# x scaled once behind the sixth projection, and values and gates taken from PSUM by ScalarE

## What is computed

```python
u = rms_norm_2(h, norm_mix_g)                  # h * rsqrt(mean(h^2) + eps) * g
proj = u @ w_in                                # 1024 -> 3744 columns
conv_in, c_q, c_kv, k_rope_raw, gate_logits = jnp.split(proj, cut, axis=-1)
a, gt = jnp.split(conv_in, 2, axis=-1)
z = a * jax.nn.sigmoid(gt)                     # 512 channels, then 31 taps each
z = silu(layer_norm(depthwise_conv(z, conv_w) + conv_b))
conv_out = z @ w_conv_out
# c_q (384) and c_kv (256) are normed and projected to 8 heads' q, k, v
mla_out = causal_attention(...) @ w_mla_out
gates = jax.nn.sigmoid(gate_logits)            # 2 x 1024
h = h + (gates[0] * conv_out + gates[1] * mla_out) @ w_out
```

## Time and profile before

| | us |
|---|---|
| median of 3 runs (2503.04 to 2503.13) | 2503.06 |
| the profiled execution | 2503.1 |
| its span, first to last instruction | 2501.3 |
| TensorE busy | 2486.5 |
| VectorE busy | 1988.3 |
| ScalarE busy | 1244.2 |
| GpSimd busy | 305.2 |

### The profile page before, as it was taken

How to read it: one execution, slowest core, us unless ns; L and a number is a source line. 1 busy time by engine, 2 the same in 40 slices (tenths; PEclk the granted TensorE clock), 3 DMA queues, 4 the chain that set the end, 5 groups by cost and what they waited for, 6 DMA issues and landing times.

```text
span 2501.3 us, 36450 instructions
## 1 busy us (share of the span) xinstructions
PE 2486.5 (99%) x14212; PEld 2185.6 (87%) x14212; DVE 1988.3 (79%) x2830; ACT 1244.2 (50%) x1975; POOL 305.2 (12%) x250
## 2 busy tenths in 40 slices
PE   8999999999999999999999999999999999999998
PEld 7999988889999889999888899998888888888887
DVE  7878867778888688887777888876899786788873
ACT  6444444444444454444554544445577535654552
POOL 4000001220000000000023100000187221200002
PEclk9999999999999999999999999999999999999999
DMA  5333332233333323334323233334333333233331
GB/s 157 99 96 99 102 104 85 78 89 98 102 101 109 110 84 100 104 97 122 99 63 93 80 104 97 110 105 136 84 75 79 126 93 110 84 108 105 101 100 59
DMA packets 487297, 246.83 MB, mean 99 GB/s; under 512 B 42321, under 2 KB 483926, under 8 KB 486870
## 3 DMA queue, kind: packets, MB, share of 16 engines
q1 hardware_dynamic: 486674, 244.19, 33.9%
q10 hardware_dynamic: 452, 0.32, 0.0%
HBM read 240.27 MB, written 4.19 MB: 98 GB/s over the span
## 4 chain that ended last, share of the span: by engine, by line
PE 97%; DVE 1%; ACT 1%; DMA 0%; issue 0%; DVEq 0%; ACTq 0%
PE bank L893 8%; PE bank L892 8%; PE bank L891 8%; PE bank L774 6%; PE bank L775 6%; PE bank L776 6%; PE psS L913 5%; PE psS L914 4%; PE psS L915 4%; PE bank L1452 3%; PE psT L957 2%; PE psT L959 2%; PE psT L958 2%; PE psT L774 2%; PE psT L775 2%; PE psT L776 2%
## 5 line engine op out<-in xcount | busy, mean ns | idle before, releaser
L2267 DVE TENSOR_TENSOR wlo<-raw,whi 128x1024 fp32r<-128x1024 f32 (+2 forms) x212 | 288.8, 1364 | 49.8 <-ACT whi L1582 46.0
L774 PE MATMUL bank<-xhl,whi 128*128 128x512 f32 x672 | 264.5, 394 | 0.0
L775 PE MATMUL bank<-xhl,whi 128*128 128x512 f32 x672 | 261.9, 390 | 0.0
L776 PE MATMUL bank<-xhl,wlo 128*128 128x512 f32 x672 | 261.8, 390 | 0.0
L891 PE MATMUL bank<-xshl,whi 128*128 128x256 f32 x840 | 237.8, 283 | 0.0
L892 PE MATMUL bank<-xshl,whi 128*128 128x256 f32 x840 | 237.7, 283 | 0.0
L893 PE MATMUL bank<-xshl,wlo 128*128 128x256 f32 x840 | 237.7, 283 | 0.0
L1582 ACT ACTIVATE whi<-raw 128x1024 fp32r<-128x1024 f32 (+2 forms) x209 | 214.5, 1029 | 37.3 <-PE bank L776 22.2
L2330 DVE TENSOR_TENSOR wlo<-tw,whi 128x1024 fp32r<-128x1024 f32 x140 | 171.5, 1225 | 63.6 <-ACT whi L1622 63.5
L913 PE MATMUL psS<-hhi,whi 128*128 128x512 f32 x488 | 191.7, 393 | 0.0
L914 PE MATMUL psS<-hlo,whi 128*128 128x512 f32 x488 | 191.6, 393 | 0.0
(11 more groups left out here) (703 smaller groups left out, 7092.2 us busy)
## 6 DMA issues: line engine op xcount, KB each, us to landing
raw<-in_ffn_wg SPq DMA_DIRECT2D x88, 512.0 KB
raw<-in_ffn_wu SPq DMA_DIRECT2D x88, 512.0 KB
raw<-in_w_in SPq DMA_DIRECT2D x53, 512.0 KB
raw<-in_w_mlp SPq DMA_DIRECT2D x40, 512.0 KB
raw<-in_ffn_wd SPq DMA_DIRECT2D x48, 256.0 KB
raw<-in_ffn_wd SPq DMA_DIRECT2D x24, 448.0 KB
raw<-in_ffn_wd SPq DMA_DIRECT2D x48, 192.0 KB
raw<-in_ffn_wd SPq DMA_DIRECT2D x48, 128.0 KB
```

Source lines behind the costliest of these rows:

```text
L774: pe.matmul(dest, a, rhs_hi(k), start=start and k == 0, stop=False)
L775: pe.matmul(dest, a, rhs_lo(k), start=False, stop=False)
L776: mm = pe.matmul(dest, b_, rhs_hi(k), start=False, stop=stop and k == tiles - 1)
L2267: dve.tensor_tensor(wlo[:, a:a + n], raw[:, a:a + n], whi[:, a:a + n].bitcast(F32), ALU.subtract).then_inc(s_split, 1)
```

## The change

- Behind kr, the sixth projection, `x` gets its inverse root after all: GpSimd multiplies the eight chunks of `x` by `inv` into `gate_a`, ScalarE rounds them with the gain into `xhi` (`scaled_hi`, as soon as kr is through with that chunk), VectorE makes `xlo` (`scaled_lo`).
- a0 waits for `scaled_lo` chunk by chunk. From it on, results in PSUM are final.
- The 24 evictions of a, g and gates leave VectorE. ScalarE takes them out of PSUM: a Copy times 0.5 for values, the Tanh itself for gates and g. `s_ea` takes the place of `s_i2` for them. Some takes get further waits (for the use of their target by others).
- On VectorE the add of the kv latents' squares stands between `scaled_lo` 0 to 3 and 4 to 7, and these stand before the three `latent_norm` and the split of a1.
- In the slots ScalarE takes the slot's own unit behind the Exp and three tap products (from slot 15 on behind the layer norm's Silu and rounding), where it used to do the Tanh of the previous slot's.
- Semaphores of the first block's attention are used again in the cross attention and for `mem`, in place of seven of their own.

```diff
             in_unit("kv", 1)
             pe.wait_ge(s_i2, evicted("q", 0))
-            in_unit("kr", 0)
+            c = unit_of("kr", 0)
+            pe.wait_ge(s_split, c + 1 + RING)
+            for k in range(KC):
+                wh, wl = wcols(whi, c, k), wcols(wlo, c, k)
+                pe.matmul(bank_of[("kr", 0)], wh, chunk(xhi, k), start=k == 0, stop=False)
+                pe.matmul(bank_of[("kr", 0)], wh, chunk(xlo, k), start=False, stop=False)
+                pe.matmul(bank_of[("kr", 0)], wl, chunk(xhi, k), start=False, stop=k == KC - 1
+                          ).then_inc(s_kc if k < KC - 1 else s_used, 1)
             pe.wait_ge(s_gn, GN2)
             pe.wait_ge(s_v7, 8 + QC + KVC - 2)
             ones_sum(psS[:, 512:1024], [chunk(lsq, QC)]).then_inc(s_ss, 1)
             pe.wait_ge(s_i2, evicted("q", 1))
-            in_unit("a", 0)
+            in_unit("a", 0, ready=lambda k: pe.wait_ge(s_xsl, k + 1))
...
                 if s % 2 == 0 and h < H2:
-                    pe.wait_ge(s_i2, evicted(*FILL[s]))
+                    pe.wait_ge(s_ea, taken(*FILL[s]))
                     project(h, "k")
...
+            def take(kind, i):
+                act.wait_ge(s_used, unit_of(kind, i) + 1)
+                dest = {"a": tmp[i % 2][:, :], "g": tmp[2 + i % 2][:, :], "gate": gate[i]}[kind]
+                if kind in ("a", "g") and i >= 2:
+                    act.wait_ge(s_z, i - 1)
...
+                act.activation(dest, bank_of[(kind, i)], ACT.Copy if kind == "a" else ACT.Tanh, scale=0.5).then_inc(s_ea, 1)
+
+            def scaled_hi(k):
+                if k < KC - 1:
+                    act.wait_ge(s_kc, k + 1)
+                else:
+                    act.wait_ge(s_used, unit_of("kr", 0) + 1)
+                act.wait_ge(s_t, k + 1)
+                act.activation(chunk(xhi, k), chunk(gate_a, k), ACT.Copy,
+                               scale=gains[:, FINAL1 * KC + k:FINAL1 * KC + k + 1]).then_inc(s_xsh, 1)
...
             split(unit_of("kr", 0) + AHEAD, 0)
+            for k in range(KC):
+                scaled_hi(k)
             for j in range(QC):
                 latent_hi(j)
...
                 products(some)
-                if s >= 3:
-                    i = s - 3
-                    act.wait_ge(s_i2, evicted("gate", i))
-                    act.activation(gate[i], gate[i], ACT.Tanh, scale=0.5).then_inc(s_gt, 1)
-                elif s == 2:
-                    glu_tanh(3)
                 if s:
                     products(some)
+                if s < LN_Y:
+                    take(*FILL[s])
...
+            def scaled_lo(k):
+                dve.wait_ge(s_xsh, k + 1)
+                dve.scalar_tensor_tensor(chunk(xlo, k), chunk(gate_a, k), gains[:, FINAL1 * KC + k:FINAL1 * KC + k + 1],
+                                         chunk(xhi, k).bitcast(F32), ALU.mult, ALU.subtract).then_inc(s_xsl, 1)
...
             newton(LATQ, acc)
             evict("kv", 1)
+            for k in range(KC // 2):
+                scaled_lo(k)
+            dve.wait_ge(s_lq, QC + KVC)
+            dve.tensor_tensor(chunk(lsq, QC), chunk(lsq, QC), chunk(lsq, QC + 1), ALU.add).then_inc(s_v7, 1)
+            for k in range(KC // 2, KC):
+                scaled_lo(k)
             for j in range(QC):
                 latent_norm(j)
             split(unit_of("kr", 0) + AHEAD, 0)
-            dve.wait_ge(s_lq, QC + KVC)
-            dve.tensor_tensor(chunk(lsq, QC), chunk(lsq, QC), chunk(lsq, QC + 1), ALU.add).then_inc(s_v7, 1)
             evict("kr", 0)
...
+            pool.wait_ge(s_inv, FINAL1 + 1)
+            for k in range(KC):
+                pool.tensor_tensor(chunk(gate_a, k), chunk(x, k), inv[:, :], ALU.mult).then_inc(s_t, 1)
```

## The result

| | before | after |
|---|---|---|
| median of 12 runs each (lowest to highest), us | 2503.03 (2502.61 to 2503.13) | 2508.59 (2505.81 to 2509.81) |
| the profiled execution and its span, us | 2503.1, 2501.3 | 2508.56, 2506.8 |

The ratio is 1.0023, with a 95% interval of 1.0015 to 1.003: 5.6 us more, inside the range and 2.8 us above the forecast. By the prediction's own bound of 2508.1 this is slower by a hair, 0.22%, where it gave 0.83 to no change ("same"); the interval takes in both. The runs of after also lie further apart than those of before, 4 us against 0.5. That turned out to be part of the answer.

A forecast was written before the change was run, and what follows sets the result against it. TensorE was taken to bound the kernel. From 2503.1 us, +1.9 (order at the sum) + 0.7 (contention) + 0 (later splits) + 0.1 (slots) gave 2505.8 us, 0.11% more; range 2502.7 to 2510.0.

The forecast's parts named there:

- What bounds the kernel: Whole kernel: TensorE bounds it at 0.227 us a matmul; less VectorE work gives back at most about 0.5 us.
- Part 1: Evictions of a, g and gates moved from VectorE to ScalarE: 0 us on the path, only slack for VectorE.
- Part 2: Sum behind kr: the add of lsq stands behind scaled_lo 0 to 3, so TensorE's sum moves by 1.9 us.
- Part 3: GpSimd's eight multiplications contend with VectorE ahead of the sum behind kr: 0.7 us, bounds 0 to 5.7.
- the last split or step adds 0.1: Weight split at 1761.33 or the root's first step behind it: meeting the end of GpSimd's work adds 0.1 us.
- pace 0.227 throughout: TensorE's matmuls keep starting 0.227 us apart everywhere; a changed pace would make the prediction wrong.
- Part 4: VectorE's later splits for g1 and v0: cost 0, with thin margins of 1.0 and 1.1 us.
- Part 5: Even slots, where the head's k waits for ScalarE's take, tightest in slot 4: 0.1 us, bound 0.6.
- (a): Rival: the stall at the sum behind kr doesn't appear; 2502.6 to 2503.3 us, chance 0.13.
- (b): Rival: VectorE was the true bound and TensorE speeds up, 11 us less; 2492 us, chance 0.02.
- (c): Rival: late takes block the heads in seven even slots, 4 to 9 us; 2510 to 2515 us, chance 0.09.
- (d): Rival: GpSimd contention at its upper bound, plus 1 us each at g1 and v0; 2509 to 2512, chance 0.08.

The follow-up runs named there:

- the takes alone: Changed kernel with x left unscaled and the add of lsq ahead of the latent norms, ScalarE's takes kept: 2504.16 us, ratio 1.0002.
- two: Changed kernel with the add of lsq behind two low parts of x in place of four: 2506.14 us, ratio 1.0013.
- no GpSimd: Changed kernel without GpSimd's eight multiplications of x; ScalarE and VectorE read x itself: 2507.21 us, ratio 1.0014.
- the take ahead of the product: Changed kernel with ScalarE's take in the slots moved ahead of the third tap product: 2508.59 us, ratio 1.002.
- the short adds: Changed kernel with GpSimd's 60 adds of tap products cut to one column of 512: 2507.12 us, ratio 1.0015.
- eight: Changed kernel with the add of lsq behind all eight low parts of x in place of four: 2511.27 us, ratio 1.0033.

## Why the prediction was near, and where it was off

**What bounds the kernel** held. TensorE's pace was the right measure, and 24 evictions less on VectorE gave nothing (the takes alone).

**Part 1**, cost 0 for the evictions, held on the path of the front. A take from PSUM lasts 0.57 to 0.60 us against the 0.60 assumed.

**Part 2**, the order, held to the tenth: forecast 1.9 us, and without GpSimd's work the wait went from 0.2 to 2.1. The chain of times held as well: the first low part was put at 1767.6, and started at 1767.43 without GpSimd's work and at 1768.59 with it. kr's chunks never held ScalarE back.

**Part 3**, contention, was right in its mechanism and 0.4 us low. The adds of `lsq` grew by 1.24 us of the 1.92 allowed, the splits by at most 0.07, so that path stayed covered. The last step was the mis-sized term: "the last split or step adds 0.1" came out as 1.1, since GpSimd was busy until 1763.59 and the root's first step began at 1762.37. Its start lay within the last multiplication, and it waited that one out and took 1.78 us. The argument had let the two share and counted a part for the overlap, while its own row at 1947.38 already ends 0.55 us behind GpSimd's. Part 2 and 3 together make 3.1 us, forecast 2.6.

**What the sum left out** is the clock. The prediction said "pace 0.227 throughout" and named a change of the pace as what would make it wrong; that is what happened, in most executions. It priced an idle stretch of 3 us at 3 us. It cost 1.6 more, and in some executions nothing more. Nothing in the trace of before shows a fall behind so short a gap in this stretch, because there was no such gap in it. A warning was there at the end of that trace, where the last matmul ends at 2494.46 us and the clock falls while the engine stands idle:

```profile
2494.50:2498.00 3.50, 0.00 (x0) 0.00 (x0) 1.24 (x2) 0.94 (x2) 0.00 (x0) 1.00 0.99 401
2498.00:2501.30 3.30, 0.00 (x0) 0.00 (x0) 0.00 (x0) 0.00 (x0) 0.00 (x0) 0.53 0.52 212
```

**Part 4** held: cost 0. The margins came out as 2.7 us at g1 (the split ends at 1788.3, TensorE starts at 1791.0) and 2.8 at v0, where 1.0 and 1.1 were forecast, because TensorE was later than thought. The warning that the cover is thin was confirmed from the other side: take away the wait at the sum and g1 waits for 1.8 us.

**Part 5** was low: 0.9 us in the profiled run, 0.1 in the other, against 0.1 with a bound of 0.6. The wait it named (slot 4, the head's k, for the take) is there with 0.2 us. The larger one, for the exponentials of slot 3, it did not see, since it followed only ScalarE's queue and not VectorE's split beside GpSimd's adds. The bound of 0.6 was passed by 0.3.

**The sum**, from before's 2503.1: -0.2 + 3.1 + 1.6 + 0.9 = 2508.5, and the profiled run took 2508.56. Without the fall of the clock it is 2505.9, next to the forecast of 2505.8; but that is the rarer execution (3 of 23 runs), so the nearness says little. Of the rivals, (a) and (b) did not occur; (c) occurs in one slot of seven with a third of its price; (d) had the contention and not the margins. The range held the time because (c) and (d) widened it, and for neither of their reasons.

## What to carry to other kernels

A wait put in front of an engine that never idled costs more than its length if the granted clock falls behind it, so look at the granted clock in the stretch after every new gap; where the gap can't go, filling it with useless matmuls took up to 2.3 of 5.6 us off here. When an order on one engine is put right, look at what the stall had hidden: here the next split was 1.8 us late behind it. And relief of an engine is worth what its waits cost others, which the waits showed as nothing, while the work that bought the relief slowed a step on the path by 1.1 us. Here, too, kernels of different groups had befores 0.6 us apart; take small differences to the kernel before of the same group. When GpSimd gets work beside VectorE, look for a step with two SBUF inputs that starts while GpSimd's instruction runs, and count the rest of that instruction, not a share of it.

## What the hardware showed that was not expected

- The granted clock fell from 1.00 to half behind idle times of 1.9, 2.1 and 3.3 us, in the profiled runs of "two", "no GpSimd" and after, and not in another run of after with 3.2 us of idle time. With 5.9 us of idle time it fell within the wait, for 6.8 us. The Trainium skill (TensorE: Matmul & The Clock Gate, Part 1: The HAM clock gate) says that a monitor sets the array's clock to one of two levels by how busy the array has been; the two levels are what the rows show. Why some executions escape is not settled by any run here, nor is the third group of after's runs near 2509.7 us, of which there is no profile.
- The longer the idle time, the fewer executions escape, if the groups of times are read as with and without a fall (a profile shows it for one or two of a kernel): five of ten at 1.9 us of idle time, three of ten at 2.1, seven of 43 at 3.2 to 3.3 (after, the take ahead of the product, the short adds), none of five at 5.9. All nine executions near 2509.7 us (two of them with the take ahead of the product) list a mean clock of 0.998 as "eight" does, and all that escaped in after 0.999; a longer fall would fit, and isn't shown.
- The cost depends on how much work lies in the low stretch: 1.6 us in after, 1.4 with a fall twice as long of which some 3.9 us were idle.
- Contention is uneven, and by turns. Beside the same multiplications the root's first step grew from 0.68 to 1.78 us and the two adds from 1.49 to 2.73, but the two splits only from 1.22 to 1.29 and 1.25; beside an add in slot 3 a split took 1.92 in one execution, and in another the add took 3.18 and the split 1.21. In the rows followed above, one waits the other's instruction out; which one was mostly a matter of who started first. Reads of PSUM stayed at 0.69 (the eviction at 1757.06).
